# A hybrid encoder on one core: side products led across phase ends, attention operands loaded and turned a phase earlier

## What is computed

```python
for l in range(DEPTH):                       # 2
    h = rmsnorm(x, norm_g[l])
    proj = einsum('bsd,de->bse', h, w_in[l])
    (a_q, a_k, a_v, a_z, b_q, b_k, b_v, b_z,
     c_qkv, c_z, c_b, c_a, gate_logits) = split(proj, offsets)
    o_a = windowed_gqa(a_q, a_k, a_v, a_sink[l], cos, sin)        # band of 128, 8 heads, 2 key heads
    y_a = (o_a * silu(a_z)) @ w_bo_a[l]
    o_b = diff_attention(b_q, b_k, b_v, lam, ...)                  # full, 4 heads, two softmaxes
    y_b = (o_b * silu(b_z)) @ w_bo_b[l]
    c_q, c_k, c_v = split(silu(conv5(c_qkv)))
    o_c = rmsnorm(gated_delta(c_q, c_k, c_v) + reversed gated_delta, c_norm_g[l])
    y_c = (o_c * silu(c_z)) @ w_bo_c[l]
    x = x + (g0 * y_a + g1 * y_b + g2 * y_c) @ w_out[l]            # g: sigmoid of gate_logits
return rmsnorm(x, final_g)
```

## Time and profile before

| | before |
|---|---|
| median of 3 runs | 2816.32 us (2814.80 to 2816.42) |
| profiled execution, its own time | 2818.19 us |
| span of the profiled execution | 2816.4 us |
| mean granted TensorE clock | 0.982 of 2.4 GHz |
| HBM read and written | 248 MB and 130 MB |

### The profile page before, as it was taken

One profiled execution on the slowest core, in us unless ns is written; L12 is line 12 of the kernel. 1 busy time (PEld: TensorE's weight loads), 2 busy tenths in 40 slices (PEclk: granted clock), 3 DMA queues, 4 the chain that ended last, 5 costly groups with the idle time before them and its releaser, 6 DMA issues. The chain is left out here.

```text
span 2816.4 us, 39100 instructions
## 1 busy us (share of the span) xinstructions
PE 2684.4 (95%) x15158; PEld 2143.7 (76%) x15158; DVE 1473.7 (52%) x1835; ACT 1153.8 (41%) x1914; POOL 1199.6 (43%) x1108
## 2 busy tenths in 40 slices
PE   8989999999999999999999999899999999999998
PEld 4867767777778789878767777677777887897786
DVE  5136527777467343476240555277764764335752
ACT  3124424666365414342121344266663653244311
POOL 2464335443365450253434653444433654303633
PEclk9999999999999999999999999999999999999999
DMA  6253224231355555754243532433224564567532
GB/s 210 92 150 98 90 80 125 90 98 68 120 184 185 187 156 155 233 187 129 83 153 105 143 104 69 123 97 98 83 68 135 191 197 160 164 161 257 158 120 105
DMA packets 394072, 380.89 MB, mean 135 GB/s; under 512 B 90144, under 2 KB 332448, under 8 KB 393888
## 3 DMA queue, kind: packets, MB, share of 16 engines
q1 hardware_dynamic: 354912, 296.39, 34.8%
q10 hardware_dynamic: 38976, 82.00, 7.9%
HBM read 248.22 MB, written 130.09 MB: 134 GB/s over the span
## 5 line engine op out<-in xcount | busy, mean ns | idle before, releaser
L266 PE MATMUL pair<-h_hi,w_hi 128*128 128x512 f32 x1792 | 740.2, 413 | 75.0 <-PEq L203 39.9
L266 PE MATMUL pair<-h_lo,w_hi 128*128 128x512 f32 x1792 | 708.5, 395 | 0.0
L266 PE MATMUL pair<-h_hi,w_lo 128*128 128x512 f32 x1792 | 708.3, 395 | 0.0
L246 POOL TENSOR_TENSOR w_hi<-w_stage,masks 128x256 fp32r<-128x256 f32 x312 | 257.5, 855 | 642.7 <-PE pair L266 604.7
L266 PEld LDWEIGHTS pair<-h_hi,w_hi 128*128 128x128 f32 x1792 | 342.4, 191 | 197.0 <-issue 83.3
L266 PEld LDWEIGHTS pair<-h_hi,w_lo 128*128 128x128 f32 x1792 | 342.4, 191 | 75.6
L266 PEld LDWEIGHTS pair<-h_lo,w_hi 128*128 128x128 f32 x1792 | 343.3, 192 | 70.2 <-issue 5.3
L281 ACT ACTIVATE ev<-pair 128x512 f32<-128x512 f32 x224 | 132.8, 593 | 456.7 <-PE pair L266 455.7
L251 POOL TENSOR_TENSOR w_lo<-w_stage,w_hi 128x256 fp32r<-128x256 f32 x312 | 247.3, 823 | 6.1
L1691 POOL TENSOR_TENSOR w_lo<-w_stage,w_hi 128x256 fp32r<-128x256 f32 x128 | 149.5, 1197 | 170.5 <-ACT w_hi L1805 170.5
L1446 ACT ACTIVATE diff_p<-pair,diff_stat 128x1024 f32<-128x1024 f32 x128 | 142.9, 1117 | 126.4 <-DVE diff_stat L1549 122.4
(11 more groups left out here) (288 smaller groups left out, 4894.7 us busy)
## 6 DMA issues: line engine op xcount, KB each, us to landing
w_stage<-in_w_in SPq DMA_DIRECT2D x132, 512.0 KB, 4.2
proj<-ev ACTq DMA_DIRECT2D x132, 512.0 KB, 2.7
gate<-proj SPq DMA_DIRECT2D x48, 512.0 KB, 3.7
prep_x<-proj SPq DMA_DIRECT2D x24, 512.0 KB, 4.1
resid<-xT SPq DMA_DIRECT2D x16, 512.0 KB, 6.2
diff_vx<-proj SPq DMA_DIRECT2D x16, 512.0 KB, 3.2
prep_g<-gc_rows SPq DMA_DIRECT2D x16, 512.0 KB, 5.0
qd_t<-prep_eg SPq DMA_DIRECT2D x16, 512.0 KB, 2.6
```

The lines of the kernel that those rows point to most:

```text
L246: last = nc.gpsimd.tensor_tensor(w_hi[s][:, part], w_stage[s][:, part], bcast(ones, PIECE), ALU.mult)
L266: last = nc.tensor.matmul(bank(self.banks[half]), a[s][:, c, :], b[:, c, w], start=(c == 0 and n == 0), stop=(c == KC - 1 and n == 2))
```

## The change

1. **Led halves.** Half 0 of the next phase's side products is computed at the end of a phase, behind its last half, by a new function `lead`, into the bank given by `LEAD_WINDOW`, `LEAD_FULL` or `LEAD_GATES` (6, 0, 6). This is so at four junctions: projection to banded, banded to full, full to preparation, preparation to delta rule. The next phase starts with half 1; its ScalarE evacuates half 0 first. `side_sum` starts one higher.
2. **Banks.** `Side` takes a list `early` of banks for the first halves: (6, 7, 5) in the banded, (0, 7, 5, 7) in the full attention.
3. **Weight 1 presplit everywhere.** Full attention (`split(17)`) and preparation (`low(17)`, with ScalarE's `high(17)`) split the second weight of the next phase as well; the starts of the banded attention, the preparation and the delta rule no longer split weight 1.
4. **Banded operands in the projection.** Loads, sine and cosine products, sums, high and low parts of operands 0 to 2, and the load of `VX`, move to the end of `project`. There GpSimd's sine products stand between the split of pair 4 and that of pair 5; ScalarE's high copies behind its last evacuation.
5. **First head's loads in the banded attention.** Both operands of head 0 and their swapped copies are loaded by SyncE behind weight 14. The preset of the preparation's semaphores moves behind the first head's sine products.
6. **Places.** Banded: FIRST 4 to 3, LAST 3 to 2, two fewer shared steps; full: FIRST 3 to 4, LAST 5 to 4. Preparation, first head: halves 1 to 4 before the keys' sum, 5 and 6 before the products, 7 between the turning of keys and values; ScalarE's evacuation of half 7, and with it `high(5)`, now stands before the copy of the turned values. Delta rule: nine halves before the first block product, evacuation of half 0 first.

```diff
+        def lead(pe, into):
+            for c in range(KC):
+                for n, (a, b) in enumerate(((w_hi, h_hi), (w_hi, h_lo), (w_lo, h_hi))):
+                    nc.tensor.matmul(bank(into), a[0][:, c, :], b[:, c, 0:HALF], start=(c == 0 and n == 0),
+                                     stop=(c == KC - 1 and n == 2))
...
@@ project, sync @@
+                    for s in range(2):
+                        sp.wait_ge(q[f"put{s}"], START + 16 * 3)
...
+                    for r in range(3):
...
+                            sp.dma_start(into, src).then_inc(q[f"win_in{r}"], 16)
+                        for a in range(4):
...
+                            sp.dma_start(win_xr[r][32 * a:32 * a + 32, :], src).then_inc(q[f"win_in{r}"], 16)
+                    sp.dma_start(win_vx[:], proj[U_AV]).then_inc(q["win_v"], 16)
...
@@ project, gpsimd @@
-                    with pool.Fori(2, pairs_of_units + 1) as i:
+                    with pool.Fori(2, pairs_of_units) as i:
                         for s in range(2):
                             split(i, s)
+                    pool.wait_ge(q["tables_in"], START + 48)
+                    for r in range(3):
+                        pool.wait_ge(q[f"win_in{r}"], START + (96 if r == 0 else 80))
+                        nc.gpsimd.tensor_tensor(win_xr[r][:], win_xr[r][:], sin[:], ALU.mult).then_inc(q["win_sin"], 1)
+                    for s in range(2):
+                        split(pairs_of_units, s)
...
@@ project, tensor @@
+                    pe.wait_ge(q["w_lo0"], START + pairs_of_units + 1)
+                    lead(pe, LEAD_WINDOW)
...
@@ project, scalar, behind the last evacuation @@
+                    for r in range(3):
+                        act.wait_ge(q["win_rot"], START + r + 1)
+                        nc.scalar.activation(win_hi[r][:], win_x[r][:], ACT.Copy).then_inc(q["win_hi"], 1)
...
@@ attend_window @@
-                FIRST, LAST = 4, 3
-                shared = (6, 10, 14, 18, 22, 26, 30)
+                FIRST, LAST = 3, 2
+                shared = (6, 12, 17, 22, 27)
...
                     weights(14)
+                    sp.wait_ge(q["z_gate"], START + 4)
+                    sp.wait_ge(q["side_put0"], START + 16 * 3)
+                    for n, (x, xr) in enumerate(((full_x[0], full_xr[0]), (full_x[1], full_xr[1]))):
+                        u = (U_BQ, U_BK)[n]
+                        sp.dma_start(x[:], proj[u]).then_inc(q["next_x"], 16)
+                        for a in range(4):
+                            r = 32 * (a ^ 1)
+                            sp.dma_start(xr[32 * a:32 * a + 32, :], proj[u, r:r + 32, :]).then_inc(q["next_x"], 16)
                     weights(15)
...
-                    side_half(0)
-                    side_half(1)
                     turn_values()
-                    side_half(2)
-                    side_half(3)
+                    for n in range(1, FIRST):
+                        side_half(n)
...
-                    side_half(tail_half(2))
+                    pe.wait_ge(q["side_lo"], START + UNITS + 1)
+                    lead(pe, LEAD_FULL)
...
@@ attend_full @@
-                FIRST, LAST = 3, 5
+                FIRST, LAST = 4, 4
...
                     for n in range(2):
                         sine(0, n, XR0[n])
+                    set_signals("prep")
...
                     split(16)
+                    split(17)
...
-                    side_half(tail_half(4))
+                    pe.wait_ge(q["side_lo"], START + UNITS + 1)
+                    lead(pe, LEAD_GATES)
...
@@ prepare, gpsimd @@
-                    low(1)
...
+                    low(17)
...
@@ prepare, tensor @@
-                        half(0)
-                        half(1)
-                        if h == 0:
-                            half(2)
-                            half(3)
+                        if h:
+                            half(0)
+                            half(1)
+                        else:
+                            for n in range(1, 5):
+                                half(n)
                         total(h, 1)
-                        half(2 if h else 4)
+                        half(2 if h else 5)
                         total(h, 0)
-                        half(3 if h else 5)
-                        half(4 if h else 6)
+                        half(3 if h else 6)
+                        if h:
+                            half(4)
                         products(h)
...
-                        if h:
-                            half(5)
+                        half(5 if h else 7)
...
+                    lead(pe, LEAD_GATES)
...
@@ prepare, scalar @@
-                        if h:
-                            out_half(h, 5)
+                        out_half(h, 5 if h else 7)
                         to_tokens("v", v_tok[:, h, :], 0.5, h)
-                        if h == 0:
-                            out_half(0, 7)
...
@@ delta_rule @@
-                    for n in range(EARLY):
+                    for n in range(1, EARLY):
                         side_half(n)
```

140 lines of the change are left out of this document (80 added, 60 removed).

## The result

| | before | after |
|---|---|---|
| median of the runs, us | 2816.4 (2814.8 to 2820.0) | 2786.0 (2784.1 to 2788.3) |
| profiled execution, us (its span) | 2818.2 (2816.4) | 2786.6 (2784.8) |
| ratio, 95% interval | | 0.989 (0.988 to 0.991) |

The change makes the kernel 1.1% faster, 2786 against the 2783 forecast.

A forecast was written before the change was run, and what follows sets the result against it. TensorE, busy 95%, was taken to bound the kernel, so only standstill and low clock could be saved. Gains less losses were 15.7 us in layer 0 and 17.5 in layer 1, together 33.2, giving 2783 us; range 2764 to 2799.

The forecast's parts named there:

- the two new waits: Waits of TensorE at the second head's norm sum (4 us) and first block product (6 us), low clock behind both.
- a pause behind the projection above 3 us: Sign of being wrong: the pause between projection and banded attention, forecast at 2.0 us, exceeds 3 us.
- more waits for evacuations inside the full attention's heads: Sign of being wrong: TensorE waits more often for evacuations within the heads of the full attention.
- Junction 1: Projection to banded attention: pause 2.0 us, half 4 at 26.3 us; gain 13.0 us in layer 0, 14.1 in layer 1.
- VectorE subtracts the third until 152.2, or 153.3: Projection's end: third low part done at 152.2 us, or 153.3 where GpSimd shares VectorE's time; TensorE restarts after 7.5 us.
- Half of the window's gain is lost: Rival, chance 0.14: sines or copies end later, projection's end moves 5 us, clock drops; 7 us lost per layer, 2797.
- Junction 2: Banded to full attention: led half covers the split of weight 17, TensorE restarts after 7.2 us; gain 8.5 us per layer.
- Full attention: End of the full attention: two halves no longer share a bank back to back; gain 0.7 us per layer.
- the DMA issues between the exponentials: Rival, chance 0.06: evacuations with 0.45 us issues lengthen full-attention waits past 2 us; 6.4 us per head, all eight 2834.
- Junction 3: Full attention to preparation: first head's chain starts 2.3 us later, new wait 4.2 us; loss 4.2 in layer 0, 3.5 in layer 1.
- The dearer table switch: Rival, chance 0.03: ScalarE's table switches on the preparation's chain cost more than the 1.28 us load; 2789.
- Junction 4: Preparation to delta rule: first block product still waits for the solved blocks, pause 6 us; loss 2.3 us per layer.

The follow-up runs named there:

- high_on_scalar: Changed kernel with ScalarE making the high parts of the projection's two last weights, and those of operands 0 and 1 before its last evacuation: 2775.2 us.
- unlead2: Changed kernel without the leading half between banded and full attention, half 0 computed behind the boundary: 2802.2 us, ratio 0.996.
- mend_led: Changed kernel, leading halves kept: weight 5 loaded early, half 1 evacuated before the keys' tanh, gated output in quarters, operands' high parts before the last evacuation: 2780.2 us.
- j3: Changed kernel with the full attention to preparation boundary undone: no leading half, no presplit of weight 17, old order of the first head: 2776.6 us, ratio 0.987.
- w5: Changed kernel with SyncE loading weight 5 ahead of head 0's stores in the preparation: 2778.9 us, ratio 0.988.
- j4: Changed kernel without the leading half between preparation and delta rule, half 0 computed behind the boundary: 2784.3 us, ratio 0.989.
- (b): Half 1 evacuated before the keys' tanh in the preparation, one of four edits made together to the changed kernel: 2780.2 us for all four.
- pieces: Changed kernel with GpSimd's two last weight splits and three sine products in the projection cut into quarters of 128x256: 2786.6 us, ratio 0.991.

## Why the prediction was right, and where not

The forecast of 2783 was met at 2786, and the two new waits came where they were named. But the prediction also named signs of being wrong, and two of them came: a pause behind the projection above 3 us (3.83), and more waits for evacuations inside the full attention's heads (seven of over half a microsecond instead of five). Both trace back to one thing that was under-booked, how much VectorE and GpSimd slow each other. All below is measured on layer 0, each from the same two events as in the prediction.

**Junction 1: 13.0 predicted, 10.9 measured.** Half 4 starts 29.6 us behind the last product (147.6 to 177.3) where 38.8 + 1.7 stood before. The mis-sized term is the pause: 2.0 booked, 3.83 measured, so that TensorE restarts 9.3 us behind the last product and not 7.5. That is 1.8 of the 2.1 us; from there to half 4 it is 20.3 us, where 18.8 and 1.2 for the clock make 20.0. The step that failed is "VectorE subtracts the third until 152.2, or 153.3": it took the 1.76 us row for the worst that GpSimd's company can do. That row stood beside instructions of 128x256; beside 128x1024 it is 3.4. The rows fit engines that take turns by whole instructions, and high_on_scalar bears this out. The Trainium skill, in "SBUF — State Buffer", section "Who interferes with whom", calls the ports that VectorE and GpSimd share an exclusive lock and says that an instruction of VectorE with two SBUF inputs contends with one of GpSimd that reads SBUF. The traces agree (1.2 us alone, 3.4 beside a GpSimd instruction of 2.4). By it the three low parts would have been booked as the sum of both engines' work. The rival "Half of the window's gain is lost" gave this reason, but put it at the sine products: the split behind them ends at 146.5, still ahead of the last product (147.6), though 1.2 us ahead and not 3.

**Banded attention: nothing predicted, 3.2 measured**, from half 4 to the last half. Of these 1.5 us are short waits that are gone, the longest 0.94 us at 309.30 of the kernel before. Another 1.5 is no gain but work that stands elsewhere: one more score group (0.55 us) ahead of half 4, and the last value sums (0.94 us, from 400.09 to 401.03) behind the last half. The prediction charged the one to junction 1 and the other to junction 2 (its 1.1) and took neither out of the stretch between. No run tests the 1.5 us of waits.

**Junction 2: 8.5 predicted, 9.1 measured** (27.2 us from the last half to the first scores before, 23.6 after, with one half of 5.45 more in them). The pause is 0.30 as said; unlead2 shows the leading half to be 7.3 us of it.

**Full attention: +0.7 predicted, some -0.8 measured.** The heads lose 1.0 us each for two of them. The rival had put this on the DMA issues between the exponentials; the waits at the evacuations that were there before grew by 0.1 us only, from 1.16 to 1.26. The cause is junction 1's again: the mix of probabilities ran beside GpSimd's gated output, which in the kernel before it did not (no mix took over 1.77 us there). The first two rows are after, the third mend_led.

```profile
542.87 3.20 DVE L1626 SCALAR_TENSOR_TENSOR diff_p<-diff_p,diff_stat,diff_p 128x1024 f32<-128x1024 f32 x1
...
542.59 2.40 POOL L1316 TENSOR_TENSOR diff_o<-diff_o,diff_zt 128x1024 f32<-128x1024 f32 x1 [2.42 <-DVE diff_o L1573]
```
```profile
542.86 1.53 DVE L1633 SCALAR_TENSOR_TENSOR diff_p<-diff_p,diff_stat,diff_p 128x1024 f32<-128x1024 f32 x1
```

Once that is in quarters (mending (c)) the mix takes 1.53 us, the pause of 1.02 us at 550.12 is gone, and 1.8 us per layer come back.

**Junction 3: -4.2 predicted, -5.7 measured**, and 4.9 by j3. The phase starts 6.15 us behind the last half (6.3 booked), the sum comes 68.3 behind that (66.9), and half 10 ends 10.4 us behind the sum's start instead of 7.6, so the clock took 2.8 (2.5). The named wait is 4.74 us where 4.2 was booked. The waits at halves 3 and 4, predicted as 1.9 each, came as 1.59 and 1.65, and a third of 1.36 us at half 8 wasn't foreseen; none of the three adds to the sum's time, since TensorE waits for the chain anyway. Right was the reason, that the chain hangs on the phase's start, and its last link: w5 moves it. The mis-sized term is the chain behind the values' silu. The silu starts 42.4 us into the phase, as booked (42.6). But the first tap behind it ran beside a whole instruction of GpSimd (783.39 to 786.77); before, it ran beside quarters. First before, then after:

```profile
804.70 1.22 DVE L1885 TENSOR_SCALAR k_all<-prep_x,prep_w 128x1024 f32<-128x1024 f32 x1
```
```profile
784.45 2.88 DVE L1938 TENSOR_SCALAR k_all<-prep_x,prep_w 128x1024 f32<-128x1024 f32 x1
```

With the four stores taking 4.22 us to issue (3.25 before), the load of weight 5 left 59.8 us into the phase and not 58.1 as before, let alone earlier; it then landed faster, and 1.4 us were left of the delay. This is read from the rows; no run takes it away alone. The dearer table switch can be dropped: the load of 1.28 us at 780.59 is followed by the tanh at 781.88, 1.29 us after its start, and the silu behind it was on time.

**Junction 4: -2.3 predicted, -1.3 measured.** The wait for the solved blocks is 6.11 (6 predicted), the boundary's pause 0.30; j4 gives 0.4 by the same events. None of these is a gain. Behind half 11, which the change does not touch, layer 0 is 2.2 us shorter; most of it comes at the delta rule's last wait, 2.44 us with the lower clock behind it before and 1.88 without after, and was not aimed at.

**Sum.** From the projection's start to the merge: 17.6 us in layer 0 (15.7 predicted), 18.0 in layer 1 (17.5). Taken from that: 1.3 us, since the projection starts later in layer 0 for a late load of `x`, and 1.1 and 1.5 us in the stage between the layers and the last one, which the change doesn't touch. 17.6 + 18.0 - 1.3 - 1.1 - 1.5 = 31.7, the spans' difference is 31.6. The forecast was 2.9 us off, but its terms in layer 0 were off by -2.1 (junction 1), +3.2 (banded attention), +0.6 (junction 2), -1.5 (full attention), -1.5 (junction 3), +1.0 (junction 4) and +2.2 (behind half 11). That they nearly cancel is luck; that junctions 1 and 2 pay and 3 and 4 don't is not.

## What to carry to other kernels

Work pulled ahead of a phase's boundary pays where the boundary waits for another engine (junctions 1 and 2: 6 and 7 us per layer), and costs where the next wait hangs on the phase's start (junction 3 with its new order: 5 us) or merely moves the wait (junction 4: 0); so follow the chain behind the boundary to its first late link before putting something in front of it. Where VectorE and GpSimd both work from SBUF behind the last product, count their instructions as one queue, and shorten it by handing one to ScalarE; at junction 1 an earlier start and cutting in quarters won nothing. In the full attention, where VectorE was awaited and GpSimd was not, cutting GpSimd's instruction gave 1.8 us per layer. And mend one link at a time: three of the waits taken away here came back elsewhere (w5: 1.92 and 1.99 us for 4.74; (b): 3.64 for 3.24; pieces: 3.04 and 1.56 for 3.83).
